# Turning the first three band results with VectorE block transposes and ScalarE copies instead of TensorE

## The reference, cut to what matters

```python
def band_attention_mixer(h, k, v, w_in, rel_table, w_out):
    qz = h @ w_in
    q = qz[..., :B_WIDTH].reshape(Bn, S, B_HEADS, B_DH)
    z = qz[..., B_WIDTH:]
    o = chunk_band_attention(q, k, v, rel_table)   # softmax(q k' * scale + bias) v, 256 tokens
    y = o.reshape(Bn, S, B_WIDTH) * jax.nn.silu(z.astype(F32))
    return y.astype(h.dtype) @ w_out
```

## Time and profile before

| | |
|---|---|
| median of 3 runs | 2407.74 us (2407.58 to 2408.61) |
| the profiled execution | 2407.68 us, span 2405.9 us |
| busy, TensorE matmul | 2389.5 us, 99% of the span |
| busy, TensorE weight load (beside the matmuls) | 1948.7 us, 81% |
| busy, VectorE | 1746.5 us, 73% |
| busy, ScalarE | 1312.5 us, 55% |
| granted TensorE clock, mean | 0.999 |

### The profile page before, as it was taken

The page is one execution under the profiler, slowest core; times in us unless marked ns, Lnnn a source line. Parts: engine busy times, 40 slices in busy tenths (PEclk is TensorE's granted clock), DMA queues, the critical chain, the costliest instruction groups (busy, mean ns, idle before and its releaser), DMA issues.

```text
span 2405.9 us, 30632 instructions
## 1 busy us (share of the span) xinstructions
PE 2389.5 (99%) x11049; PEld 1948.7 (81%) x11049; DVE 1746.5 (73%) x2436; ACT 1312.5 (55%) x1911; POOL 45.1 (2%) x65
## 2 busy tenths in 40 slices
PE   9999999999999999999999999999999999999998
PEld 7777888888888888778888888888888778888887
DVE  8885778677787776668778677677776676666665
ACT  6665465545553555555545544545455576655553
POOL 1100000000000000000000000000000000000000
PEclk9999999999999999999999999999999999999999
DMA  8445889788889897477777787777777457776654
GB/s 297 145 132 173 271 291 309 256 303 303 284 314 307 289 318 229 158 229 241 239 235 234 243 271 242 238 235 236 240 240 241 154 186 267 249 242 213 227 192 139
DMA packets 161831, 578.14 MB, mean 240 GB/s; under 512 B 18289, under 2 KB 20593, under 8 KB 161681
## 3 DMA queue, kind: packets, MB, share of 16 engines
q1 hardware_dynamic: 160432, 572.64, 71.4%
q0 software_dynamic: 1104, 3.28, 0.4%
q10 hardware_dynamic: 144, 0.26, 0.0%
HBM read 574.01 MB, written 2.10 MB: 239 GB/s over the span
## 4 chain that ended last, share of the span: by engine, by line
PE 94%; DVE 2%; ACT 2%; DMA 1%; issue 1%; POOL 0%; SPq 0%; DVEq 0%; ACTq 0%
PE PS L1171 30%; PE PS L1173 30%; PE PS L1172 30%; DVE WL L2206 1%; ACT WH L1563 1%; PE PS L914 1%; DMA X<-in_x 0%; PE PS L809 0%; PE PS L882 0%; DVE X L2173 0%; PE PS L1004 0%; PE PS L1072 0%; PE PS L1024 0%; PE PS L1025 0%; PE PS L1021 0%
## 5 line engine op out<-in xcount | busy, mean ns | idle before, releaser
L2206 DVE TENSOR_TENSOR WL<-W,WH 128x1024 fp32r<-128x1024 f32 x814 | 988.5, 1221 | 509.9 <-ACT WH L1563 503.9
L1563 ACT ACTIVATE WH<-W 128x1024 fp32r<-128x1024 f32 x814 | 855.1, 1058 | 723.6 <-PE PS L1173 681.0
L1171 PE MATMUL PS<-WH,XTH 128*128 128x512 f32 x2144 | 853.7, 398 | 2.8 <-DVE XTL L1718 1.2
L1173 PE MATMUL PS<-WH,XTL 128*128 128x512 f32 x2144 | 835.7, 390 | 0.0
L1172 PE MATMUL PS<-WL,XTH 128*128 128x512 f32 x2144 | 835.1, 389 | 0.0
L1171 PEld LDWEIGHTS PS<-WH,XTH 128*128 128x128 f32 x2144 | 402.7, 188 | 93.7 <-issue 11.4
L1173 PEld LDWEIGHTS PS<-WH,XTL 128*128 128x128 f32 x2144 | 402.5, 188 | 85.4
L1172 PEld LDWEIGHTS PS<-WL,XTH 128*128 128x128 f32 x2144 | 402.9, 188 | 83.8 <-issue 3.8
L1171 PE MATMUL PS<-WH,YTH 128*128 128x512 f32 x1120 | 440.2, 393 | 3.5 <-DVE WL L2206 2.4
L1173 PE MATMUL PS<-WH,YTL 128*128 128x512 f32 x1120 | 436.2, 389 | 0.0
L1172 PE MATMUL PS<-WL,YTH 128*128 128x512 f32 x1120 | 436.1, 389 | 0.0
(11 more groups left out here) (286 smaller groups left out, 1192.6 us busy)
## 6 DMA issues: line engine op xcount, KB each, us to landing
W<-in_vec SPq DMA_DIRECT2D x192, 512.0 KB, 4.5
W<-in_avoz SPq DMA_DIRECT2D x192, 512.0 KB, 4.5
W<-in_wg SPq DMA_DIRECT2D x88, 512.0 KB, 5.1
W<-in_wu SPq DMA_DIRECT2D x88, 512.0 KB, 4.9
W<-in_wd SPq DMA_DIRECT2D x88, 512.0 KB, 4.9
W<-in_gate SPq DMA_DIRECT2D x64, 512.0 KB, 4.6
W<-in_aqk SPq DMA_DIRECT2D x64, 512.0 KB, 4.7
W<-in_aout SPq DMA_DIRECT2D x64, 512.0 KB, 4.4
```

What stands on the lines that cost most here:

```text
L1171: e.matmul(p, x, WH[:, g % NH, j], start=first, stop=False)
L1173: i = e.matmul(p, y, WH[:, g % NH, j], start=False, stop=last)
L1563: e.activation(WH[:, n % NH], W[:, i % NW], ACT.Copy).then_inc(s_hi, 1)
L2206: e.tensor_tensor(l, src, h.bitcast(F32), ALU.subtract).then_inc(s_lo, 1)
```

## The change

band(j) for j = 0, 1, 2 no longer turns its result on TensorE. TensorE's task ends after the last pv. VectorE waits for its own last scaling and makes blocks_T(ZG) in calls 31 and 32, and pair_lows in calls 43 and 44. ScalarE makes the 16 copies of quadrants in calls 33 to 40, two in each, and pairs_T in calls 41 and 42. The gate copy of the next band, which overwrites ZG, waits for the block transposes instead of the TensorE ones. Band 3's result and all queries are turned as before.

```diff
+TQ_BAND, MT_BAND, N_BAND = 23, 19, 3
@@ tensor_program, band
                 yield from band_order(score_, turn, pv, lambda: j in zdone)
+                if j < N_BAND:
+                    return
                 yield from ticks(4)
                 banks = [take(("bT", j, a)) for a in range(2)]
@@ scalar_program, gate_z
                 if j:
-                    w.wait_ge(*filled(("bT", j - 1, 0)))
-                    w.wait_ge(*filled(("bT", j - 1, 1)))
+                    w.wait_ge(s_tq, TQ_BAND + j)
@@ scalar_program, band
                 yield from band_order(score_, turn, pv, lambda: j in zdone)
+                if j < N_BAND:
+                    yield from ticks(4)
+                    yield from quadrants(TQ_BAND + j + 1, MT, 2, s_mt)
+                    w.wait_ge(s_unit, free)
+                    yield from pairs_T(MT_BAND + j + 1, 4 * j, None)
+                    return
                 yield from ticks(4)
@@ vector_program, band
                 yield from band_order(score_, turn, pv, lambda: j in zdone)
+                if j < N_BAND:
+                    yield from ticks(2)
+                    w.wait_ge(s_bo, 4 * j + 4)
+                    yield from blocks_T(ZG)
+                    yield from ticks(10)
+                    yield from pair_lows(4 * j, None)
+                    return
                 yield from ticks(4)
```

## The result

The changed kernel takes 2417.85 us (median of 6 runs, 2416.09 to 2418.15), the kernel before 2407.66 us in the same comparison. The ratio is 1.0041 with a 95% interval of 1.0031 to 1.0051: the change makes the kernel slower by about 10 us, twice the forecast 5.1 us. The direction was forecast, but the time lies outside the range of the forecast (2411 to 2414.5 us) and above 2416.5 us, the top of all that the prediction allowed for. The profiled execution took 2418.05 us, span 2416.2 us.

The account below looks back on a forecast made before the run. TensorE's instruction list was taken to bound the kernel (busy 2389.5 of 2405.9 us): 2407.68 minus 2.52 for removed transposes plus 7.6 for waits gives 2412.8 us, range 2411 to 2414.5.

Parts of the forecast that it names:

- what is removed: TensorE at the ends of bands 0 to 2: three groups of 16 small transposes leave, 0.84 us each, 2.52 us gained.
- the wait at the first scores: TensorE at three band boundaries waits for ScalarE's second query copy: 2.4, 2.4 and 2.7 us, 7.6 us lost in all.
- The end of ScalarE's list: Second query copy done at T = 12.7, 12.7 and 13.0 us, counted from the query chunk's end; scores wanted it at 10.4.
- what else the delay could reach: Weights, VectorE's query copy, first head's exponentials and weight tiles' DMA after each boundary: taken as 0 us.
- found room in a wait of VectorE: VectorE gets 1.3 us more work in each band; it had waited 2.30 us in front of the old rests.
- Rival 3: Delay paid more than once, TensorE waiting again at line 1080: 1 to 1.5 us more a boundary, about 2416; 0.18 with another rival.
- The reserve of 2 us at line 1080: TensorE turns the first head's exponentials; with 1 us more on both engines, 2 us of reserve was said to stay.
- The query transposes' wait of 0.5 us: TensorE's 16 query transposes wait 0.5 us for VectorE's late query copy, counted inside the 2.4 us wait.
- a falling clock: Sign that the forecast is wrong: the granted clock of a stretch around the query chunk's end, 1.00 before, falls.
- The rule against the change: Skill's advice of TensorE for full turns: 0.84 us there against 1.30 on VectorE and 6.84 on ScalarE; queue decides, not work.

## Why the prediction was wrong

**Right: what is removed.** 0.84 us a group was forecast, 0.86 to 0.88 came out at every boundary and in every kernel that could show it.

**Right: the wait at the first scores, its cause and nearly its size.** The end of ScalarE's list was put at T = 12.7 and came at 12.9; 7.6 us were forecast for three waits and 8.1 found. (The prediction's own terms, 2.4 and 2.4 and 2.7, add up to 7.5; the slip changes nothing.) Four kernels confirm the cause: with one copy of 16 no wait, with an earlier start a shorter one by as much, with the copies alone the whole loss, with six fewer copies ahead none.

**Wrong: the term "what else the delay could reach" at 0.** The prediction looked at the weights, at VectorE's query copy and at line 1080, and found reserves. It did not look at line 1092 in the middle of the band (1093 after), which has 0.2 us of reserve. It cost 1.4 us in band 1. VectorE's rests in calls 43 and 44, for which the prediction found room in a wait of VectorE at another place (2.30 us in front of the old rests), stand in this chain: it is 2.9 us late in front of them and 3.5 behind. Rival 3 had the mechanism, a delay paid more than once, at 1 to 1.5 us a boundary, but named the wrong line and gave it less than 2 in 10. The reserve of 2 us at line 1080 was real. But a reserve measured at one consumer says nothing of the next one: the links from the query copies over the first heads, the gate copy and the third head's exponentials to the second head's softmax weights hang on each other, and the whole chain has the reserve of its tightest end. The query transposes' wait of 0.5 us was seen and was rightly put inside the other.

**Wrong: the clock.** The prediction named a falling clock as a sign of error and gave it no price. It cost 3.2 us, more than the whole gain of the transposes. The prediction could have seen the danger in the trace before. There the last matmul starts at 2398.50 and ends at 2398.89, TensorE has nothing more to do, and the granted clock falls about 2.4 us later, about the length of the waits that were forecast (columns as above):

```profile
2400.50:2401.00 0.50, 0.00 (x0) 0.00 (x0) 0.40 (x2) 0.00 (x0) 0.04 (x1) 1.00 0.06 16
2401.00:2401.50 0.50, 0.00 (x0) 0.00 (x0) 0.50 (x2) 0.00 (x0) 0.00 (x0) 0.82 0.00 0
2401.50:2402.00 0.50, 0.00 (x0) 0.00 (x0) 0.50 (x2) 0.00 (x0) 0.00 (x0) 0.50 0.00 0
```

The pace at the lower clock could have been read there too: the first matmuls of ones, of the same 128x512, start 0.43 us apart (1.79, 2.22 and 2.64 us, line 1125) instead of 0.23, so that nearly half the length of a slow stretch is lost. How long a stretch lasts behind such a wait no row before could show; in the changed kernel the two cost 1.70 and 1.47 us. With a term from 0 to some 1.6 us, as seen afterwards, for each of the three waits, and with the 1.4 us, the range would have ended above 2418.

**The balance.** -2.6 + 8.1 + 1.4 + 3.2 = 10.1 by the two profiles, against -2.5 + 7.6 + 0 + 0 = 5.1.

**The rule against the change.** The prediction said that the queue decides, and not the sum of work. That held. The turn on TensorE was the faster one for the change as made, but the larger work by itself did not make it so: by the traces the same work in places with reserve gave the 0.87 us a band back, for bands 0 and 1.

**Open:** what decides whether a wait of 2.5 us brings the clock down; which part of the 1.04 us in band 3 (seen where TensorE was not slow before it) is ScalarE's copies and which VectorE's rests; and whether band 2's result has any order in which it can be turned without loss. None was found in the four complete kernels that turn it by blocks.

## What to carry to other kernels

Work moved off the engine that never idles is free only if the engine that takes it has time between what it last got and what it must next deliver; count everything that stands ahead of the next deadline in its in-order queue, and put the added work behind it. An engine's idle time in front of an instruction that waits for another waiting engine is no reserve: follow the chain of turns to its first consumer on the bound engine, and take the smallest margin on the way. A wait of the matmul engine costs more than its length when the clock falls behind it, so price it at both clock levels.

## What the runs showed of the hardware

- A wait of TensorE of 2.2 to 4.2 us in a stream of matmuls went in six of seven profiled cases with a stretch at granted clock 0.5, in which 128x512 matmuls started 0.43 us apart instead of 0.23. The stretch cost 1.5 to 1.7 us, and 2.4 us with the longest wait. The exception was a wait of 2.47 us. With waits of 1.4 to 1.8 us no such stretch was seen in seven profiled cases.
- At the end of the kernel before, the last matmul ends at 2398.89; the granted clock was 1.00 until 2401.0, 0.82 in the next half microsecond and 0.50 from 2401.5.
- Ten matmuls of ones with unused results in a wait of 2.4 to 2.7 us kept the clock at 1.00 and made the boundary 1.3 to 1.6 us faster; in a wait of 1.8 us, behind which the clock had not fallen, they cost 0.2 us.
- A slow stretch of TensorE can hide another loss: the engines that feed it catch up meanwhile. With the slow stretch in band 3 removed, a wait of 0.8 us for a weight tile appeared that was not there before.
